# Two edits to a two-block fp32 layer on one core: a new order of the opening loads and squares, and another bank for a gate tile at the last attention pair

## The reference, cut to what matters

```python
c_act = silu(c)
mod = c_act @ w_ada + b_ada              # 1024 x 6144: shift, scale, gate, twice
shift1, scale1, gate1, shift2, scale2, gate2 = split(mod, 6)
h = rmsnorm(x, g_norm1) * (1 + scale1) + shift1        # x: 512 x 1024, fp32
q, k, v, rq, rk, rv, rg, br = split(h @ w_in)
# stick-breaking attention, 16 heads of 64, causal
z = q @ k.T / 8
log_a = log_sigmoid(z) + (reverse cumsum of log_sigmoid(-z) over earlier columns)
o_sb = where(mask, exp(log_a), 0) @ v
o_ret = silu(rg) * head_rmsnorm(retention(rotary(rq), rotary(rk), rv))
g_sb, g_ret = split(sigmoid(br + b_branch))
merged = g_sb * (o_sb @ w_proj_sb) + g_ret * (o_ret @ w_proj_ret)
x = x + gate1 * (merged @ w_out)
# then a gated FFN, and a second block (delta rule, conv, cross attention, conv FFN)
```

## Time and profile before

| what | us |
|---|---|
| median of 3 runs | 2095.3 |
| the three runs | 2092.92, 2095.3, 2098.51 |
| the profiled execution, its own time | 2093.45 |
| its span | 2091.7 |
| TensorE busy | 2046.9 |
| VectorE, ScalarE, GpSimd busy | 926.8, 891.8, 896.1 |
| mean granted TensorE clock | 0.997 |

### The profile page before, as it was taken

How to read it: one execution, slowest core, us unless ns; L and a number is a source line. 1 busy time by engine, 2 the same in 40 slices (tenths; PEclk the granted TensorE clock), 3 DMA queues, 4 the chain that set the end, 5 groups by cost and what they waited for, 6 DMA issues and landing times.

```text
span 2091.7 us, 27936 instructions
## 1 busy us (share of the span) xinstructions
PE 2046.9 (98%) x10078; PEld 1674.3 (80%) x10078; DVE 926.8 (44%) x1175; ACT 891.8 (43%) x1095; POOL 896.1 (43%) x412
## 2 busy tenths in 40 slices
PE   8999999999999999999999999999999989999998
PEld 4888878787878788888888878779798778888887
DVE  3254542454545454511112337877571256555313
ACT  4466653232323233433332247677653335444321
POOL 3222224343434344344444446759265134444453
PEclk9999999999999999999999999999999999999999
DMA  8222213424242423233323322210144122323331
GB/s 317 71 61 61 61 31 115 171 77 169 79 167 79 167 81 101 81 99 92 99 92 101 110 91 72 80 61 1 66 146 131 41 81 88 103 91 100 100 101 61
DMA packets 56383, 203.78 MB, mean 97 GB/s; under 512 B 6256, under 2 KB 8432, under 8 KB 54896
## 3 DMA queue, kind: packets, MB, share of 16 engines
q1 hardware_dynamic: 56304, 202.70, 29.9%
HBM read 200.57 MB, written 2.10 MB: 97 GB/s over the span
## 4 chain that ended last, share of the span: by engine, by line
PE 76%; issue 8%; DVE 5%; POOL 5%; ACT 5%; DMA 0%; POOLq 0%; DVEq 0%; SPq 0%; ACTq 0%
PE acc L2028 18%; PE acc L2030 17%; PE acc L2029 17%; PE aux L2028 4%; PE aux L2030 4%; PE aux L2029 4%; POOL w_lo L524 3%; POOL cfy L549 2%; ACT sp L583 2%; PE acc L2318 2%; PE aux L2213 1%; DVE qkvf L1701 1%; PE aux L2216 1%; PE aux L2308 1%; PE aux L2230 1%
## 5 line engine op out<-in xcount | busy, mean ns | idle before, releaser
L524 POOL TENSOR_TENSOR w_lo<-raw,w_hi 128x1024 fp32r<-128x1024 f32 x317 | 771.9, 2440 | 1142.5 <-ACT w_hi L583 1141.7
L583 ACT ACTIVATE w_hi<-raw 128x1024 fp32r<-128x1024 f32 x317 | 335.3, 1060 | 540.5 <-PE acc L2030 411.4
L2028 PE MATMUL acc<-x_hi,w_hi 128*128 128x512 f32 (+1 forms) x1336 | 525.8, 394 | 13.0 <-DVEq L1172 6.0
L2029 PE MATMUL acc<-x_lo,w_hi 128*128 128x512 f32 (+1 forms) x1336 | 517.3, 387 | 0.0
L2030 PE MATMUL acc<-x_hi,w_lo 128*128 128x512 f32 (+1 forms) x1336 | 517.2, 387 | 0.0
L2028 PEld LDWEIGHTS acc<-x_hi,w_hi 128*128 128x128 f32 x1336 | 251.3, 188 | 71.6 <-DVEq L1172 10.4
L2030 PEld LDWEIGHTS acc<-x_hi,w_lo 128*128 128x128 f32 x1336 | 251.1, 188 | 51.9
L2029 PEld LDWEIGHTS acc<-x_lo,w_hi 128*128 128x128 f32 x1336 | 251.4, 188 | 49.3 <-issue 0.5
L1474 DVE TENSOR_TENSOR ht<-acc,tn 128x512 f32<-128x512 f32 x21 | 14.5, 692 | 173.8 <-PE acc L2030 171.3
L1204 DVE SCALAR_TENSOR_TENSOR adac<-ada,c_act,adac 128x1024 f32<-128x1024 f32 x28 | 40.7, 1454 | 92.9 <-DMA ada<-in_ada 92.4
L2028 PE MATMUL aux<-x_hi,w_hi 128*128 128x512 f32 x192 | 75.2, 391 | 0.8 <-POOL w_lo L524 0.8
(11 more groups left out here) (514 smaller groups left out, 3672.7 us busy)
## 6 DMA issues: line engine op xcount, KB each, us to landing
raw<-in_weights SPq DMA_DIRECT2D x324, 512.0 KB, 3.6
ada<-in_ada SPq DMA_DIRECT2D x32, 512.0 KB, 3.7
ada<-in_ada_first SPq DMA_DIRECT2D x8, 1024.0 KB, 10.7
resid<-in_x SPq DMA_DIRECT2D x2, 1024.0 KB, 7.7
out<-resid SPq DMA_DIRECT2D x16, 128.0 KB, 1.7
decay<-in_tables SPq DMA_DIRECT2D x4, 256.0 KB, 3.6
memf<-in_mem SPq DMA_DIRECT2D x1, 1024.0 KB, 5.0
angles<-in_tables SPq DMA_DIRECT2D x1, 512.0 KB, 3.9
```

The costliest lines, as they stand in the source:

```text
L524: nc.gpsimd.tensor_tensor(lo_home(u), raw[s][:], hi_home(u).bitcast(F32), ALU.subtract).then_inc(lo_ready, 1)
L583: return nc.scalar.activation(out, in_, func, **kw)
L2028: M(out, a_hi, b_hi, start=first, stop=False)
L2029: M(out, a_hi, b_lo, start=False, stop=False)
```

## The change

In the opening, SyncE issues the two halves of `x` first and `cols` behind them; `small` goes behind the fourth `ada_first` piece. A matrix of ones, `first_ones`, is made by a VectorE memset, so that `unread` (now three matmuls) and the sums of squares don't use `small`. ScalarE squares tiles 0 to 5, and takes Silu, `c_pad` and the table set behind them; VectorE squares tiles 6 and 7 and adds the squares in two pairs (4 + 5, 6 + 7), so that six matmuls sum eight tiles. The five tables from `small` are made behind the eighth `x_lo`.

At the last pair the gate tile takes `At(30)`, bank 0, and comes whole and first; ScalarE reads it out ahead of the two `probability` steps. Output tile 0 takes `At(31)`, bank 1, and is done in pieces of 3, 3 and 1 depth steps around the `log_a` blocks. Two depth steps of output tile 1 (in `aux`) come ahead of the wait for the second probability. `values` is `At(32)`. Output tiles 2 to 7 take other numbers; tile 7 is `At(37)`, bank 1.

```diff
-        SB_OUT_AT = {0: At(30), 2: At(35), 3: At(32), 4: At(37), 5: At(34), 6: At(39), 7: At(36)}
+        SB_OUT_AT = {0: At(31), 2: At(34), 3: At(33), 4: At(36), 5: At(35), 6: At(38), 7: At(37)}
...
-            sp_.dma_start(small[:], dram["small"]).then_inc(S["tables_loaded"], 16)
-            sp_.dma_start(cols[:], dram["cols"]).then_inc(S["consts_loaded"], 16)
             sp_.dma_start(resid[:, 0:half, :], dram["x"][:, 0:half, :]).then_inc(S["x_loaded"], 16)
             sp_.dma_start(resid[:, half:KT, :], dram["x"][:, half:KT, :]).then_inc(S["input_loaded"], 16)
+            sp_.dma_start(cols[:], dram["cols"]).then_inc(S["consts_loaded"], 16)
...
             load_ada(3)
+            sp_.dma_start(small[:], dram["small"]).then_inc(S["tables_loaded"], 16)
             load_ada(4)
...
-            act.wait_ge(S["consts_loaded"], 16)
-            step.own(f(c_act[:], cols[:, C0["c"]:C0["c"] + KT], ACT.Silu))
-            own["consts_ready"].next()
-            own["c_ready_act"].own(f(c_pad[:, :, 0], c_act[:]))
-            nc.scalar.preload_act_table_set("natural_log_exp_and_others")
             act.wait_ge(S["x_loaded"], 16)
-            for k in range(KT):
+            for k in range(KT - 2):
                 if k == KT // 2:
                     act.wait_ge(S["input_loaded"], 16)
                 own["rsq_ready"].own(f(x_sq[:, k, :], resid[:, k, :], ACT.Square))
-            own["consts_ready"].next(6)
+            act.wait_ge(S["consts_loaded"], 16)
+            step.own(f(c_act[:], cols[:, C0["c"]:C0["c"] + KT], ACT.Silu))
+            own["consts_ready"].next(3)
+            own["c_ready_act"].own(f(c_pad[:, :, 0], c_act[:]))
+            nc.scalar.preload_act_table_set("natural_log_exp_and_others")
...
+                def gate(p, u, t):
+                    act.wait_ge(unit_used, (u + 1).val())
+                    step.own(f(gates[:, p, :], bank(t), ACT.Identity,
+                               bias=cols[:, C0["b_branch"] + p:C0["b_branch"] + p + 1]))
+                    nc.scalar.sem_inc(acc_free[t.slot(2)], 1)
...
-                    t = At(31)
+                    gate(p, u, At(30))
                 probability(0)
                 probability(1)
                 split_hi(u + AHEAD)
-                act.wait_ge(unit_used, (u + 1).val())
...
+                if p < PAIRS - 1:
+                    gate(p, u, t)
...
+            ready.own(V.memset(first_ones[:], 1.0))
             ready.own(V.memset(c_pad[:], 0.0))
...
+            dve.wait_ge(S["input_loaded"], 16)
+            for k in (KT - 2, KT - 1):
+                step.own(V.tensor_tensor(x_sq[:, k, :], resid[:, k, :], resid[:, k, :], ALU.mult))
+            own["rsq_ready"].next(KT - 2)
+            for k in (KT - 4, KT - 2):
+                own["recip_ready"].own(V.tensor_tensor(x_sq[:, k, :], x_sq[:, k, :], x_sq[:, k + 1, :], ALU.add))
+
+            def constants():
+
+                dve.wait_ge(S["tables_loaded"], 16)
...
                 low(k)
+            constants()
...
-            free(At(38))
+            free(At(39))
...
-            pe.wait_ge(S["tables_loaded"], 16)
-            unread(2)
-            for k in range(KT):
+            own["consts_ready"].next()
+            unread(3)
+            for k in range(KT - 4):
                 own["rsq_ready"].next()
-                m = M(rs, ones, x_sq[:, k, :], start=k == 0, stop=k == KT - 1)
+                M(rs, first_ones[:, 0:P], x_sq[:, k, :], start=k == 0, stop=False)
+            for k in (KT - 4, KT - 2):
+                own["recip_ready"].next()
+                m = M(rs, first_ones[:, 0:P], x_sq[:, k, :], start=False, stop=k == KT - 2)
...
+                    gate_part(u, At(30), 0, KT)
                     own["osb_ready"].next(PAIRS - 2)
                     wait_bank(SB_OUT_AT[0])
-                    out_part(0, 0, PAIRS - 2)
-                    gate_part(u, At(31), 0, 4)
+                    out_part(0, 0, 3)
                     log_a(0)
-                    gate_part(u, At(31), 4, 7)
+                    out_part(0, 3, PAIRS - 2)
                     log_a(1)
-                    gate_part(u, At(31), 7, KT)
                     own["osb_ready"].next()
                     out_part(0, PAIRS - 2, PAIRS - 1)
+                    own["prob_ready"].next()
+                    out_part(1, 0, 2)
...
-            own["prob_ready"].next(2)
-            values(At(33))
-            out_part(1, 0, PAIRS - 1)
+            own["prob_ready"].next()
+            values(At(32))
+            out_part(1, 2, PAIRS - 1)
```

More of the change, by code:

```diff
@@ L262, in build_program @@
         gate_t = tn
-        (vw_hi, vw_lo, ada0, x_sq, ada_rows, c_pad), _ = overlay(
+        (vw_hi, vw_lo, ada0, x_sq, ada_rows, c_pad, first_ones), _ = overlay(
             over, ("vw_hi", (P, 4, UNIT), F32R), ("vw_lo", (P, 4, UNIT), F32R), ("ada0", (P, 4, KT, 2 * P), F32),
-            ("x_sq", (P, KT, T), F32), ("ada_rows", (P, 2, 2 * P), F32), ("c_pad", (P, KT, 32), F32))
+            ("x_sq", (P, KT, T), F32), ("ada_rows", (P, 2, 2 * P), F32), ("c_pad", (P, KT, 32), F32),
+            ("first_ones", (P, T), F32))
         qk_at = [norm_at, norm_at + T * 4, norm_at + 2 * T * 4, norm_at + 3 * T * 4]
@@ L710, in pair @@
                 split_hi(u + AHEAD)
-                act.wait_ge(unit_used, (u + 1).val())
-                step.own(f(gates[:, p, :], bank(t), ACT.Identity, bias=cols[:, C0["b_branch"] + p:C0["b_branch"] + p + 1]))
-                nc.scalar.sem_inc(acc_free[t.slot(2)], 1)
+                if p < PAIRS - 1:
+                    gate(p, u, t)
             for p in range(PAIRS):
@@ L720, in _ @@
                     own["tile_done"].next()
-                    own["osb_hi_ready"].own(f(osb_hi[:, PAIRS - 1, :], bank(At(33))))
+                    own["osb_hi_ready"].own(f(osb_hi[:, PAIRS - 1, :], bank(At(32))))
                 split_hi(At(U0["sb_out"] + n + AHEAD))
@@ L1191, in _ @@
             ready.own(V.memset(eps[:, 1:2], EPS * EPS))
[L1192 to L1197, removed]
+            dve.wait_ge(S["input_loaded"], 16)
[6 more added lines that the diff above has]
+                dve.wait_ge(S["tables_loaded"], 16)
+                ready.own(V.tensor_copy(negtri_r[:], sm["neg_tri"]))
+                ready.own(V.tensor_scalar(negone_r[:], sm["ones"], -1.0, None, ALU.mult))
+                ready.own(V.tensor_copy(ident_b[:], sm["ident"]))
+                ready.own(V.tensor_scalar(mask_b[:], sm["keep"], -NEG, NEG, ALU.mult, ALU.add))
+                ready.own(V.tensor_scalar(causal_b[:], sm["tri"], -NEG, NEG, ALU.mult, ALU.add))
             def ada(w, dst, k):
@@ L1302, in _ @@
                 pair(p)
-            out_lo(At(33), PAIRS - 1)
+            out_lo(At(32), PAIRS - 1)
             for n in range(PAIRS):
@@ L1452, in _ @@
             own["last_sq"].skip(2)
-            own["rsq_ready"].skip(KT)
             second(4)
@@ L2141, in modulation_sums @@
                 for n, m_ in enumerate((1, 0)):
-                    m = M(out[:, n:n + 1], ada_rows[:, k % 2, m_ * P:(m_ + 1) * P], ones[:, 0:1], start=True, stop=True)
+                    m = M(out[:, n:n + 1], ada_rows[:, k % 2, m_ * P:(m_ + 1) * P], first_ones[:, 0:1], start=True, stop=True)
                 m.then_inc(S["ada_ready"], 1)
@@ L2147, in unread @@
                 for _ in range(n):
-                    M(aux[:, 2 * T:3 * T], ones, small[:, 0:T], start=True, stop=True)
-            pe.wait_ge(S["tables_loaded"], 16)
-            unread(2)
-            for k in range(KT):
+                    M(aux[:, 2 * T:3 * T], first_ones[:, 0:P], first_ones[:], start=True, stop=True)
+            own["consts_ready"].next()
+            unread(3)
+            for k in range(KT - 4):
                 own["rsq_ready"].next()
-                m = M(rs, ones, x_sq[:, k, :], start=k == 0, stop=k == KT - 1)
+                M(rs, first_ones[:, 0:P], x_sq[:, k, :], start=k == 0, stop=False)
+            for k in (KT - 4, KT - 2):
+                own["recip_ready"].next()
+                m = M(rs, first_ones[:, 0:P], x_sq[:, k, :], start=False, stop=k == KT - 2)
             m.then_inc(S["stat_ready"], 1)
```

## The result

Five runs of the changed kernel lie between 2084.84 and 2087.04 us, median 2086.55; five of the kernel before between 2092.92 and 2098.51, median 2095.69. The ratio is 0.995 with a 95% interval of 0.9938 to 0.9962, so the change is faster by 0.38 to 0.62%. The profiled execution took 2086.55, span 2084.8: 6.9 us less in span than the profiled one of before.

A forecast was written before the change was run, and what follows sets the result against it. TensorE was taken as the bound, busy 2046.9 of 2091.7 us, so only closed gaps or fewer matmuls pay. Opening 2.4, last pair 2.9 and retention bank 1.15 sum to 6.45 off the 2095.3 median: 2088.8, range 2086 to 2091.5.

The forecast's parts named there:

- the first term: The opening, up to the first value matmul: 2.4 us sooner, bounds -0.5 and 3.0.
- the 0.3% line: Whole kernel: a change under 0.3% (6.3 us) can't be told from none; faster 0.48, same 0.48, slower 0.04.
- Landing of `x`: Opening loads: halves of `x` land near 6.9 and 9.55, 1.5 and 1.4 us sooner.
- The bound of 3.2: Upper bound in us on the earlier landing of `x`, if nothing ran ahead of need.
- Cover: TensorE before `x`: memset 0.55, six `unread` passes end at 7.1, ahead of the first square at 7.56, costing nothing.
- Sums of squares: Opening, TensorE: sums start at 7.6, wait 0.6 for the first pair, end at 13.65 instead of 16.22.
- ScalarE's two loads: Opening, behind the squares: two table loads of 1.28 us each, 0.15 exposed; the skill's 2.66 per switch doubted.
- Loads behind it: Modulation pieces land in time (first near 12.8, asked for at 13.65); five tables of 0.23 each are free.
- Last pair and retention: Last attention pair 2.9 us (bounds 1.2 and 3.1); bank at first retention tile 1.15 us (0 and 1.25).
- the count by steps: Last pair, TensorE instructions timed one by one: 310.9 instead of 313.99, 3.1 us; by gaps, 1.36 + 1.70 - 0.25 = 2.8.
- the collision of VectorE and GpSimd: Rival, value projection: six more `x_lo` beside GpSimd splits cost 7.3 us, giving 2096.1; chance 0.04.
- The other rivals: `x` no sooner (2090.3, chance 0.12); longer table loads (2091.2, 0.07); last pair's second probability or bank late (2090.4, 0.06).

## Why the prediction was off, point by point

The sum said 6.45 us off one execution, and by 1600 us there were 9.0; the forecast median of 2088.8 is 2.25 above the measured one. The mechanism of each edit was right; what failed is a size, that of the first term. The forecast lay on the 0.3% line with equal chances to either side, and the ratio's interval is beyond that line. That the profiled execution was forecast at 2087.0 and came at 2086.55 is luck: 2.1 of its 9.0 were lost again to the clock.

- **Landing of `x`: this step failed, in size.** It was put at 6.9 and 9.55, so 1.5 and 1.4 us sooner, and `x` landed at 5.81 and 8.28, 2.58 and 2.65 sooner. I took it that 0.62 MB of later transfers run ahead whatever stands in front. By 5.81 the queue had moved 5.81 x 243 = 1.41 MB, of which 1.05 were due: 0.36 ahead. The rest of the miss is the curve of bytes against time, taken over from the old order: that one reaches 1.41 MB at 6.05, so 0.85 of the 1.1 us are the smaller share ahead and 0.25 the curve. Together they are the whole miss of the opening (2.4 forecast, 3.49 measured). The bound of 3.2 covered it; the value chosen was the lower half.
- **Cover**: right. The memset took 0.48 and the six passes ended at 6.36, 0.15 ahead of the first sum at 6.51. Less room than thought: with `x` sooner by more than that, these passes would have held up the first sum.
- **Sums of squares**: right in form. Wait for the first pair 0.40 rather than 0.6, six sums' worth from 6.51 to 12.60, 6.1 us both in forecast and trace.
- **ScalarE's two loads**: right, two of 1.28, and the roots start 0.16 later than in the run without one; at the first `x_hi` nothing of that is left. That a switch costs the load alone is shown twice: 9.78 + 1.28 = 11.06 and Silu at 11.08, 11.55 + 1.28 = 12.83 and the roots at 12.85; the last square ends at 9.77, so nothing stands ahead of the load either. The Trainium skill ("ScalarE: Activation LUTs", section "What ACT_TABLE_LOAD costs") gives about 2.66 us for each switch, 1.38 of it a drain, and the trace doesn't agree. By that figure, an estimate, the first `x_hi` would have come near 19, and it came at 16.20.
- **Loads behind it**: right, no modulation piece was waited for. The five tables took 0.23 each but for two of 2.3 beside GpSimd, and nobody waited.
- **Last pair and retention**: right, 2.9 + 1.15 = 4.05 forecast and 4.16 measured. The pair gave 2.91 (from last scores to the row at 313.99 before, 306.98 after: 33.07 and 30.16), between the count by steps (3.1) and that by gaps (2.8). The bank at retention gave 1.25: 348.20 stands 1.48 behind the row ahead of it, where 0.23 is usual. The clearing of `pret` was just in time, as said: VectorE's first rotation had 1.45 idle ahead of it before and has 0.23 now.
- **Missing from the sum**: 0.36 us at 51 us. The sums of modulation there start 29.60 and 29.57 us behind the first value in the two profiles with the old opening, TensorE having waited 0.17 for `ada_rows`, and 29.22 to 29.26 in the ten with the new one in which the clock stayed up. So this is of the opening, and why is open. Another 0.5 us lie between 715 and 847, where two executions of the changed kernel differ by as much (132.1 and 132.7): not of the change as far as shown.
- **From profile to median**: I took the profiled execution's distance of 1.85 from the median as given. At 1700 us its clock was down for 6.8 us, as little as in any profile, and in the one after for twice that; by this stage, which the change doesn't touch, the two are 2.1 apart.
- **Rivals**: the collision of VectorE and GpSimd was priced for the value projection, where it stayed as it was (1.96 and 2.00 us for two `x_lo`). It was met elsewhere, in the modulation steps of retention, where one execution lost 4.4 us and not 1.2: a chain with 0.6 us to spare and then the clock stand behind it. The other rivals didn't occur.

## What to carry to other kernels

Where a load is moved to the front of a queue, its landing can't be read off the byte curve of the old order: that curve is made by the very loads that go. Take a gain from a profile as the distance between rows that answer to each other in the last stage that the change reaches, not as the difference of spans: here these are 9.0 and 6.9. A tile whose bank the tile before it used costs its read-out, here 1.2 us each time, and a wait behind the engine's own sequencer ("issue") is found by asking which semaphore stands in front of the instruction and what gives it.

## What the runs showed of the hardware that was not expected

- A TensorE idle of 1.3 to 3.0 us is sometimes followed by a stretch at 0.50 of the clock, and sometimes not. Behind the idle of 1.25 to 1.29 us at 31 to 36 us the clock fell in four of sixteen profiled executions, and in none of the three of the changed kernel; ahead of the first `rsc` product it fell behind 2.42 us and not behind 2.23. In such a stretch matmuls of 128 x 512 come 0.43 us apart instead of 0.23.
- The transfers of 320 KB and 257.5 KB ahead of 1 MB delay it by 0.5 and 0.3 us alone, about the 0.44 by which it is issued later, and by 2.4 together, where it is issued 0.9 later.
- A VectorE instruction from and to SBUF that started 0.08 us behind a GpSimd split took 2.87 us instead of 0.75; started 0.21 ahead of the split it took 0.75, and the split 2.79 instead of 2.39. A 128 x 128 cast beside a split took 2.3 instead of 0.23.
